# Second block's last linear layer by token halves: one in plain fp32 ahead of the row gathers, the other among the mixes

## The chip, the cores and the metric

The kernel runs on one core of one Trainium2 chip. The metric is the device time of one execution in microseconds (us), the median of several runs. Five engines work side by side, each on its own list of instructions and in order: TensorE (PE in the profile; PEld is its loading of weights), VectorE (DVE), ScalarE (ACT), GpSimd (POOL) and SyncE (SP). They wait for one another through semaphores only. Transfers are issued from SP (weights) and from POOL (gathered rows) into queues of their own, and the same 16 DMA engines serve both.

## The reference, cut to what matters

Two transformer blocks over 256 tokens of width 1024; the second block ends with a product-key expert layer (`peer`). What the change touches:

```python
# second_block, 256 tokens, D = 1024
merged = g_m * (y_m @ w_branch_mlstm) + g_l * (y_l @ w_branch_lru)
x = x + merged @ w_out                     # the last linear layer ahead of peer
h2 = rms_norm(x, norm2_g)
x = x + peer(h2, peer_w_q, sub_keys, expert_u, expert_v)

# peer, for 8 heads, 128 keys a half, 16384 experts
q = h2 @ w_q                               # 8 heads x 2 halves x 128
scores = q . sub_keys                      # 8 x 2 x 128 a token
idx, gate = the 16 best pairs of keys of each head, softmax
act = gelu(expert_u[idx] . h2)             # a row of 1024 for each index
out = sum over 8 x 16 of gate * act * expert_v[idx]
```

Each token needs 128 rows of `expert_u` and of `expert_v`, which lie side by side in DRAM as one row of 2048 floats (8 KB).

## The kernel before, in words

Activations lie with features on the 128 partitions: `hF` (the residual, named residual in the profile), `xF` (normed) and `merged` are 8 slices of 128 features by 256 tokens. Weights come in tiles of 1024 x 256 floats (1 MB), 2048 floats a partition, into a ring of seven slots (`raw_tiles`, weight_tiles in the profile). SP loads a tile (line 1475) when the tile seven places earlier has been freed by its last PE group. Products go through eight PSUM banks, four that DVE empties ("v") and four that ACT empties ("a"); `Groups.begin` makes PE wait until the bank's earlier content is taken.

*Split layers.* Linear layers whose rounding matters run in three passes of fp32r: ACT rounds a weight tile (`round_ahead`, line 1693, the activation at 1702), DVE makes the low part (`low_ahead`, lines 2290 to 2297), and `split_group` multiplies high x high, low x high and high x low over all 256 tokens (lines 734, 735, 738): 48 matmuls a tile. The activations are split likewise. Tiles are rounded up to two tiles ahead. *Plain layers* (queries, scores, keys) run in fp32 as they are; each such matmul leaves two records in the profile.

*Order around the change.* In `merge` PE computes branch_l in four groups; DVE multiplies each by a gate and adds it to merged (lines 3080, 3082); ACT rounds merged (line 2165) and DVE makes its low part (line 3086). PE then transposes the keys (keysT; DVE copies them, line 3092) and runs `w_out` as a split layer in four groups over all tokens. DVE adds each to the residual (line 2315), scales by the norm's gain into xF (`gained_rows`, line 2324), ACT squares (line 2171).

In `peer` (PE's from line 1329) the order is: head 0's query of token half 0 (line 1341), xF turned to token-major, scores of half 0 (line 1353), the same of half 1, sums of squares (`row_sums`, line 668), head 1's query (line 1364), the residual transposed into the output banks (line 1390). Then 257 batches of two row slots. For each: POOL gathers a row for each of 128 tokens (line 1678), DVE multiplies it with the tokens and sums (line 3198), ACT takes the gelu (line 2211), DVE makes a diagonal matrix (line 3208) and PE adds diagonal x row to the output banks (`mix`, line 1401). Eight batches make a unit (one head of one token half), 16 slots; eight units make a half. Written by hand between the mixes are: queries and scores of heads 2 to 7 on PE (`query`, two halves i of 16 matmuls over 256 tokens; `scores`, line 1378), their copies on ACT (lines 2175, 2179), the choice of keys and pairs for the unit two ahead on DVE. Head 0's first eight slots of half 0 get their index early (`early_rows`, line 3124); its last instruction, line 3154, releases POOL's first gather.

*Row buffers.* There are 16 buffers of 1 MB: four places outside the weight tiles, `squares`, three places of the rounded tiles, seven raw slots and `spare_row`. A raw slot can hold rows only after its last weight tile: buffer 8 + i is the slot of the query tile i + 1. `BUF_JOINS` says at which gather a buffer joins the rotation; until then it isn't used. Gather c waits for its index, and for the mix that used its buffer last (or for the tile's release).

Of the kernel before, what the change touches and what calls it, by code (L numbers as in the profile page):

```python
# [13 lines left out]
P = 128  # L14
# [29 lines left out]
BUF_JOINS = {9: 14, 10: 26, 11: 36, 12: 54, 13: 70, 14: 88}  # L44
# [187 lines left out]
def two_blocks(nc, t, out):  # L232
    with ExitStack() as ctx:
# [243 lines left out]
        g_m, merged = view(2048, KT, SEQ, extra=True), view(6272, KT, SEQ)  # L477
# [9 lines left out]
        merged_high, merged_low = x_high, by_k(work_parts[:, 6272:6272 + KT * SEQ])  # L487
# [104 lines left out]
        merged_rounded, merged_split = sem("merged_rounded"), sem("merged_split")  # L592
# [32 lines left out]
        def _(pe):  # L625
# [34 lines left out]
            def row_sums(key, parts=4):  # L660
# [655 lines left out]

            def merge():
# [9 lines left out]
                split_linear("w_out", "v", (arrived(merged_high, merged_rounded, 2), arrived(merged_low, merged_split, 2)))  # L1327

            def peer():
                x = normed()  # L1330
                query_slot = None

                def first_query(b):

                    nonlocal query_slot
                    if b == 0:
                        query_slot = G.plain_tile()
                    bank = G.begin("a", ("first_pq", b))
                    for k in range(KT):
                        for i in range(2):  # L1340
                            mm = pe.matmul(bank[:, i * P:(i + 1) * P], weight(query_slot)[:, k, i * P:(i + 1) * P],
                                           x(k)[:, b * P:(b + 1) * P], start=(k == 0 and i == 0), stop=(k == KT - 1 and i == 1))
                    G.end(mm)
                    if b == 1:
                        G.free()

                def first_scores(b):

                    pe.wait_ge(act_took, G.took["first_pq", b])
                    pe.wait_ge(dve_took, G.took["keysT", 0])  # L1350
                    bank = G.begin("a", ("first_scores", b))
                    for i in range(2):
                        mm = pe.matmul(bank[:, i * P:(i + 1) * P], qP[:, i, b * P:(b + 1) * P], keysT[:, i, :], start=True, stop=True)
                    G.end(mm)
# [1959 lines left out]
```

## Time and profile before

| | |
|---|---|
| median of 3 runs | 2529.25 us (2522.64 to 2538.05) |
| profiled execution | 2531.99 us, span of the profile 2530.2 us |
| busy in the span | PE 2362.8 us (93%), DVE 2022.8 (80%), ACT 1254.8 (50%), POOL 296.2 (12%) |
| DMA | 786.56 MB, mean 311 GB/s; SP's queue 504.46 MB, POOL's 276.58 MB |
| chain that ended last | PE 65%, DMA 17%, DVE 12%, ACT 3%, issue 3% |

The page cuts the span into 40 slices and gives the busy share of each engine in each; the windows give the same for any stretch, with the granted TensorE clock (1.00 is full speed), the share of the 16 DMA engines and GB/s. The chain that ended last goes from the last instruction back, at each step to what released it; "issue" is time in which nothing that the profile shows was waited for. Groups by form give count, total busy time and the mean of one instruction; matmuls overlap, so the pace of many is read from the total and not from the mean.

### The profile page before, as it was taken

How to read it: one execution, taken by the hardware profiler on the slowest of the kernel's cores; microseconds unless marked ns; L12 is line 12 of the kernel's file. 1: busy time of each engine (PE TensorE's matmuls, PEld its weight loads, DVE VectorE, ACT ScalarE, POOL GpSimd, SP SyncE). 2: the span in 40 equal slices, each digit the busy share in tenths (PEclk: the TensorE clock that was granted, in tenths of full speed). 3: DMA queues.
4: the chain of work that ended last, by engine and by line, in shares of the span. 5: the costliest groups of instructions: out<-in, count | busy, mean ns of one | idle time of the engine just before them, and what ended most of it. 6: DMA issues, size and time to landing. Idle time of an engine off the chain costs nothing.

```text
span 2530.2 us, 31600 instructions
## 1 busy us (share of the span) xinstructions
PE 2362.8 (93%) x12256; PEld 1864.8 (74%) x12256; DVE 2022.8 (80%) x3044; ACT 1254.8 (50%) x1303; POOL 296.2 (12%) x305
## 2 busy tenths in 40 slices
PE   9999999999899999999999999989999987878786
PEld 8899999899788788878878888988885543323332
DVE  5866764965899999999999998686768878787875
ACT  2564433264778888887888784438422111111111
POOL 0000000000000010000000000000023443333341
PEclk9999999999999999999999999999999999989899
DMA  8554555541999999999999996532679999999997
GB/s 245 163 190 131 190 195 150 159 151 35 403 363 394 421 408 406 421 414 414 408 417 412 407 414 202 149 101 90 223 275 416 421 421 421 422 422 421 421 421 299
DMA packets 238476, 786.56 MB, mean 311 GB/s; under 512 B 24368, under 2 KB 154544, under 8 KB 162288
## 3 DMA queue, kind: packets, MB, share of 16 engines
q1 hardware_dynamic: 198000, 504.46, 53.1%
q0 software_dynamic: 39184, 276.58, 26.7%
q10 hardware_dynamic: 1136, 3.43, 0.3%
q8 instruction: 99, 1.62, 0.3%
q14 instruction: 57, 0.47, 0.1%
HBM read 777.08 MB, written 7.34 MB: 310 GB/s over the span
## 4 chain that ended last, share of the span: by engine, by line
PE 65%; DMA 17%; DVE 12%; ACT 3%; issue 3%; POOL 0%; DVEq 0%; SPq 0%; ACTq 0%
DMA dense_weights<-in_peer_rows,work 13%; PE banks L914 7%; PE banks L915 7%; PE banks L916 7%; PE banks L734 6%; PE banks L735 5%; PE banks L738 5%; PE banks L1401 5%; PE banks L780 5%; PE banks L1026 3%; PE banks L1027 3%; DVE weight_tiles_low L2671 2%; DMA weight_tiles<-in_moe_tiles 2%; PE banks L644 1%; PE banks L1040 1%
## 5 line engine op out<-in xcount | busy, mean ns | idle before, releaser
L2671 DVE TENSOR_TENSOR weight_tiles_low<-weight_tiles,weight_tiles_high 128x2048 fp32r<-128x2048 f32 x212 | 481.3, 2286 | 32.8 <-ACT weight_tiles_high L1941 29.9
L1401 PE MATMUL banks<-dense_weights,work 128*128 128x512 f32 x888 | 412.8, 615 | 56.4 <-DVE work L3208 56.3
L1941 ACT ACTIVATE weight_tiles_high<-weight_tiles 128x2048 fp32r<-128x2048 f32 x207 | 396.2, 1918 | 81.7 <-PE banks L916 50.0
L1401 PEld LDWEIGHTS banks<-dense_weights,work 128*128 128x128 f32 x888 | 172.6, 198 | 286.8 <-issue 197.2
L2297 DVE TENSOR_TENSOR weight_tiles_low<-weight_tiles,weight_tiles_high 128x2048 fp32r<-128x2048 f32 x105 | 239.6, 2288 | 130.1 <-ACT weight_tiles_high L1702 129.8
L3198 DVE CUSTOM_DVE_ANT_0 dense_weights<-dense_weights,banks 128x1024 f32<-128x1024 f32 x222 | 266.5, 1218 | 67.1 <-DMA dense_weights<-in_peer_rows,work 66.1
L2211 ACT ACTIVATE work<-work,small 128x2 f32<-128x2 f32 x129 | 38.1, 295 | 538.5 <-DVE work L3198 538.1
L1678 POOL DMA_INDIRECT dense_weights<-in_peer_rows,work x222 | 208.9, 941 | 582.5 <-DVE work L3154 311.1
L734 PE MATMUL banks<-weight_tiles_high 128*128 128x256 f32 x992 | 235.8, 282 | 5.3 <-issue 4.4
L735 PE MATMUL banks<-weight_tiles_high,weight_tiles_low 128*128 128x256 f32 x992 | 233.1, 280 | 0.0
L1702 ACT ACTIVATE weight_tiles_high<-weight_tiles 128x2048 fp32r<-128x2048 f32 x105 | 200.2, 1909 | 58.0 <-PE banks L916 29.5
L734 PEld LDWEIGHTS banks<-weight_tiles_high 128*128 128x128 f32 x992 | 189.5, 191 | 8.7 <-issue 7.3
L735 PEld LDWEIGHTS banks<-weight_tiles_high,weight_tiles_low 128*128 128x128 f32 x992 | 189.4, 191 | 0.2
L914 PE MATMUL banks<-weight_tiles_high,gathered_parts 128*128 128x512 f32 x448 | 176.8, 395 | 1.7 <-DVE gathered_parts L2682 0.9
L1026 PE MATMUL banks<-weight_tiles_high,gathered_parts 128*128 128x512 f32 x448 | 176.5, 394 | 0.0
L916 PE MATMUL banks<-weight_tiles_high,gathered_parts 128*128 128x512 f32 x448 | 175.0, 391 | 0.0
L2671 DVE TENSOR_TENSOR work_parts<-work,weight_tiles_high 128x2048 fp32r<-128x2048 f32 x59 | 134.8, 2285 | 5.6 <-ACT weight_tiles_high L1941 5.3
L1941 ACT ACTIVATE weight_tiles_high<-work 128x2048 fp32r<-128x2048 f32 x59 | 113.6, 1925 | 30.7 <-PE banks L916 20.7
L3208 DVE TENSOR_SCALAR work<-ident,work 128x128 f32<-128x128 f32 x256 | 79.1, 356 | 47.8 <-ACT work L2211 46.8
L915 PE MATMUL banks<-weight_tiles_low,gathered_parts 128*128 128x512 f32 x296 | 115.5, 390 | 0.0
L780 PE MATMUL banks<-normed,weight_tiles 128*128 128x256 f32 (+1 forms) x512 | 111.7, 380 | 0.0
L1027 PE MATMUL banks<-weight_tiles_low,gathered_parts 128*128 128x512 f32 x280 | 109.2, 390 | 0.0
(543 smaller groups left out, 4855.1 us busy)
## 6 DMA issues: line engine op xcount, KB each, us to landing
weight_tiles<-in_moe_tiles SPq DMA_DIRECT2D x216, 1024.0 KB, 14.9
work<-in_moe_tiles SPq DMA_DIRECT2D x60, 1024.0 KB, 15.2
weight_tiles<-in_w_in SPq DMA_DIRECT2D x38, 1024.0 KB, 5.5
dense_weights<-in_moe_tiles SPq DMA_DIRECT2D x30, 1024.0 KB, 15.4
spare_row<-in_moe_tiles SPq DMA_DIRECT2D x30, 1024.0 KB, 15.3
weight_tiles<-in_w_xkv SPq DMA_DIRECT2D x16, 1024.0 KB, 5.4
weight_tiles<-in_ffn_w_gate SPq DMA_DIRECT2D x11, 1024.0 KB, 5.3
weight_tiles<-in_ffn_w_up SPq DMA_DIRECT2D x11, 1024.0 KB, 5.3
```

The source lines that it names most:

```text
L734: pe.matmul(o, high[:, k, n_], high_x(k), start=(k == 0 and i == 0), stop=False)
L735: pe.matmul(o, low[:, k, n_], high_x(k), start=False, stop=False)
L780: mm = pe.matmul(bank[0:m, i * SEQ:(i + 1) * SEQ], w[:, k, i * P:i * P + m], x(k), start=(k == 0), stop=(k == KT - 1))
L914: pe.matmul(o, a_high, b_high, start=start, stop=False)
L915: pe.matmul(o, a_high, b_low, start=False, stop=False)
L916: return pe.matmul(o, a_low, b_high, start=False, stop=stop)
L1026: pe.matmul(o, pairs, high, start=start, stop=False)
L1401: mm = pe.matmul(halves[half], diag[(first + j) % 8], pair_row(first + j)[:, 1, half * 512:(half + 1) * 512], start=False, stop=end and j ...
L1941: act.activation(high_tile(g, p, par, j), raw_tile(g, p, par, j), ACT.Copy).then_inc(g.high, 1)
L2297: dve.tensor_tensor(low_tiles[:, n % RING, 0:size], raw_tiles[:, n % RING, 0:size], high_tiles[:, j % HIGH_RING, 0:size].bitcast(F32), ALU ...
L2671: dve.tensor_tensor(low_tile(g, p, par, j), raw_tile(g, p, par, j), high_tile(g, p, par, j).bitcast(F32), ALU.subtract).then_inc(g.split, 1)
L3198: ins = dve.tensor_tensor_reduce(u_row, u_row, tokens(b), 1.0, 0.0, ALU.mult, ALU.add, dots[:, c:c + 1])
```

## The change

`w_out` no longer runs as a split layer. Its first half (tokens 0 to 127) runs in plain fp32 right after the keys, tile by tile; merged isn't rounded or split. Its second half (`out_rest`, tokens 128 to 255) follows among the mixes of unit 0, one tile ahead of the first mix and three behind mixes 3, 5 and 7; each group begins with identity x residual, so that ACT can copy the bank into the residual. The four tiles stay in their slots until then. Norm sums, roots and gains go by halves too (`row_sums`, `row_std_of`, `gained_rest`, `inverse_row_std`). Heads 0 to 3 (`HALVED`) get query and scores by halves: half 0 ahead of the mixes (heads 0 and 1) and in units 0 and 1 (heads 2 and 3), half 1 in units 2 to 5, their tiles held until then; heads 4 to 7 stay whole. merged moves to another place of the work area, and the joins of the row buffers change.

```diff
-BUF_JOINS = {9: 14, 10: 26, 11: 36, 12: 54, 13: 70, 14: 88}
+HALVED, SECOND_ORDER = 4, (1, 0, 2)
+BUF_JOINS = {11: 36, 12: 54, 8: 62, 13: 70, 14: 88, 9: 96, 10: 104}
...
-        g_m, merged = view(2048, KT, SEQ, extra=True), view(6272, KT, SEQ)
+        g_m, merged = view(2048, KT, SEQ, extra=True), view(8192, KT, SEQ)
...
 # PE, row_sums: one half at a time
-                    for b in range(TB):
-                        mm = pe.matmul(bank[:, b:b + 1], squares[:, k, b * P:(b + 1) * P], ones[:, 0:1],
-                                       start=(k == 0 and b == 0), stop=(k == KT - 1 and b == TB - 1))
+                    mm = pe.matmul(bank[:, 0:1], src[:, k, :], ones[:, 0:1], start=(k == 0), stop=(k == KT - 1))
...
 # PE, merge
-                split_linear("w_out", "v", (arrived(merged_high, merged_rounded, 2), arrived(merged_low, merged_split, 2)))
+                for g in range(4):
+                    out_tiles.append((G.plain_tile(), len(G.need) - 1))
+                    bank = G.begin("v", ("w_out", g))
+                    for i in range(2):
+                        for k in range(KT):
+                            pe.wait_ge(merged_ready, k // 2 + 1)
+                            mm = pe.matmul(bank[:, i * P:(i + 1) * P], weight(out_tiles[g][0])[:, k, i * P:(i + 1) * P], merged[:, k, 0:P],
+                                           start=(k == 0), stop=(k == KT - 1))
+                    G.end(mm, ("w_out", g))
...
 # PE, peer
+                def out_rest(g):
+                    slot, tile = out_tiles[g]
+                    bank = G.begin("a", ("w_out_rest", g))
+                    for i in range(2):
+                        o = bank[:, i * P:(i + 1) * P]
+                        pe.matmul(o, ident[:, :], hF[:, 2 * g + i, P:2 * P], start=True, stop=False)
+                        for k in range(KT):
+                            mm = pe.matmul(o, weight(slot)[:, k, i * P:(i + 1) * P], merged[:, k, P:2 * P], start=False, stop=(k == KT - 1))
+                    G.end(mm, ("w_out_rest", g))
+                    G.freed[tile] = (group_done, G.total)
...
-                first_query(0)
+                first_query(0, 0)
                 tokens("v", 0)
-                first_scores(0)
-                first_query(1)
-                first_scores(1)
-                row_sums("norm2_ms")
-                query(1, 0)
-                query(1, 1)
+                first_scores(0, 0)
+                first_query(1, 0)
+                row_sums(("norm2_ms", 0), squares[:, :, 0:P], 4)
+                first_scores(1, 0)
                 halves = [out_banks("v", 0)]
+                out_rest(0)
...
 # PE, behind the mixes (part is the batch within unit u)
                     if u == 0:
-                        if part == 0:
-                            scores(1)
-                        if part < 2:
-                            query(2, part)
+                        if part == 1:
+                            first_query(2, 0)
                         elif part == 2:
-                            scores(2)
-                        elif part in (4, 6):
-                            query(3, part // 2 - 2)
-                        elif part == 7:
-                            scores(3)
+                            first_scores(2, 0)
+                        elif part in (3, 5, 7):
+                            out_rest(part // 2)
+                    elif u == 1 and part == 0:
+                        first_query(3, 0)
                     elif h < PHEADS and part in (1, 3):
+                        if u == 1 and part == 1:
+                            first_scores(3, 0)
                         query(h, part // 2)
                     elif h < PHEADS and part == 5:
                         scores(h)
+                    elif u == 1 and part == 6:
+                        row_sums(("norm2_ms", 1), squares_rest, 1)
+                    elif 2 <= u < 2 + HALVED - 1 and part == 6:
+                        first_query(SECOND_ORDER[u - 2], 1)
+                    elif 3 <= u < 3 + HALVED - 1 and part == 0:
+                        first_scores(SECOND_ORDER[u - 3], 1)
+                    elif u == PHEADS - 3 and part == 1:
+                        first_query(HALVED - 1, 1)
+                    elif u == PHEADS - 3 and part == 3:
+                        first_scores(HALVED - 1, 1)
...
 # ACT, merge
-                for g in range(4):
-                    s = slice(2 * g, 2 * g + 2)
-                    round_ahead(("branch_l", g))
-                    act.wait_ge(merged_ready, g + 1)
-                    act.activation(merged_high[:, s, :], merged[:, s, :], ACT.Copy).then_inc(merged_rounded, 1)
+                round_ahead(("branch_l", 3))
...
 # ACT, behind gelu(n)
+                    elif u == 1 and part == 0:
+                        out_rest(3)
+                        act.wait_ge(act_took, G.took["w_out_rest", 3])
+                        act.activation(squares_rest, hF[:, :, P:2 * P], ACT.Square).then_inc(sq_ready, 1)
+                        first_query(3, 0)
...
 # DVE, merge
-                for g in range(4):
-                    s = slice(2 * g, 2 * g + 2)
-                    dve.wait_ge(merged_rounded, g + 1)
-                    dve.tensor_tensor(merged_low[:, s, :], merged[:, s, :], merged_high[:, s, :].bitcast(F32), ALU.subtract).then_inc(merged_split, 1)
...
-                add_to_residual("w_out", gained_rows)
+                for g in range(4):
+                    if g > 0:
+                        gained_rows(g - 1)
+                    ready(("w_out", g))
+                    s = hF[:, 2 * g:2 * g + 2, 0:P]
+                    take(dve.tensor_tensor(s, pair(bank_of(("w_out", g)), 2, P), s, ALU.add))
+                gained_rows(3)
...
 # DVE, behind weights(n)
-                    if u == 0 and part == 1:
+                    if u == 1 and part == 0:
+                        gained_rest()
+                    elif u == 2 and part == 1:
+                        inverse_row_std(1)
+                    elif u == 0 and part == 1:
                         choose_keys(1)
```

`first_query(h, b)` is the query of head h for token half b (16 matmuls of 128 columns), `first_scores(h, b)` its scores; a halved head's tile is freed by its second half. `gained_rest` waits for ACT's fourth copy of `out_rest` and scales the second half of the residual, eight instructions of 128 x 128.

## Rows read from the trace of the kernel before

**Rows 1.** The page, the span in 40 equal slices of 63.3 us: DMA share and GB/s.

```profile
DMA  8554555541999999999999996532679999999997
GB/s 245 163 190 131 190 195 150 159 151 35 403 363 394 421 408 406 421 414 414 408 417 412 407 414 202 149 101 90 223 275 416 421 421 421 422 422 421 421 421 299
```

**Rows 2.** Windows: stretch, length, busy time of each engine, clock, DMA share, GB/s.

```profile
1821.00:1839.00 18.00, 14.72 (x114) 14.27 (x114) 14.17 (x15) 6.68 (x5) 0.00 (x0) 0.91 0.54 176
1839.00:1865.00 26.00, 25.62 (x228) 25.42 (x226) 10.39 (x33) 5.47 (x8) 0.00 (x0) 1.00 0.52 162
1876.00:1926.00 50.00, 45.57 (x169) 29.21 (x167) 40.37 (x126) 8.85 (x18) 15.96 (x17) 1.00 1.01 422
1926.00:1936.00 10.00, 9.81 (x29) 4.99 (x30) 8.60 (x20) 4.45 (x8) 4.01 (x5) 1.00 0.98 385
2100.00:2500.00 400.00, 311.26 (x657) 129.49 (x656) 315.33 (x821) 54.46 (x123) 144.99 (x154) 0.92 1.01 421
```

**Rows 3.** Chain of waits, 1827 to 1881 us: start, us, what.

```profile
1828.70 0.66 PE banks L636 x4
1829.36 3.13 issue
...
1854.34 1.81 PE banks L738 x16
1856.15 3.57 PE banks L1341 x32
...
1881.40 3.44 PE banks L1401 x8
```

**Rows 4.** Timeline of DVE: start, us, engine, line, what, idle before and its releaser.

```profile
1825.76 2.29 DVE L2297 TENSOR_TENSOR weight_tiles_low<-weight_tiles,weight_tiles_high 128x2048 fp32r<-128x2048 f32 x1 [2.51 <-ACT weight_tiles_high L1702]
1829.29 2.49 DVE L3086 TENSOR_TENSOR work_parts<-work,weight_tiles_high 128x512 fp32r<-128x512 f32 x4
1831.70 2.47 DVE L3092 COPY work<-banks 128x512 f32<-128x512 f32 x4
...
1881.43 1.22 DVE L3198 CUSTOM_DVE_ANT_0 dense_weights<-dense_weights,banks 128x1024 f32<-128x1024 f32 x1 [1.25 <-DMA dense_weights<-in_peer_rows,work]
...
1886.58 0.76 DVE L3208 TENSOR_SCALAR work<-ident,work 128x128 f32<-128x128 f32 x2 [3.92 <-ACT work L2211]
```

**Rows 5.** Groups by form, 1827 to 1875 us: line, engine, what, count, busy, mean ns.

```profile
L1341 PE MATMUL banks<-normed,weight_tiles 128*128 128x128 f32 x64 | 7.5, 275 | 0.0
L1341 PEld LDWEIGHTS banks<-normed,weight_tiles 128*128 128x128 f32 x64 | 7.3, 192 | 0.0
...
L668 PE MATMUL banks<-ones,squares 128*128 128x1 f32 x32 | 4.7, 281 | 0.0
...
L2324 DVE TENSOR_SCALAR normed<-residual,cols 128x256 f32<-128x256 f32 x8 | 2.4, 349 | 0.0
```

**Rows 6.** Timeline of PE: half a head's query over 256 tokens.

```profile
1885.56 3.62 PE L1364 MATMUL banks<-normed,weight_tiles 128*128 128x256 f32 x16
```

**Rows 7.** Timeline of SP's queue: the second, fourth, seventh and eighth query tile.

```profile
1827.27 0.37 SPq L1475 DMA_DIRECT2D weight_tiles<-in_peer_w_q  x1
...
1839.86 0.37 SPq L1475 DMA_DIRECT2D weight_tiles<-in_peer_w_q  x1
...
1856.18 0.37 SPq L1475 DMA_DIRECT2D weight_tiles<-in_peer_w_q  x1
1864.65 0.37 SPq L1475 DMA_DIRECT2D weight_tiles<-in_peer_w_q  x1
```

**Rows 8.** Timeline of POOL: gathers 0, 25 and 255.

```profile
1865.81 1.00 POOL L1678 DMA_INDIRECT dense_weights<-in_peer_rows,work  x1 [311.11 <-DVE work L3154]
...
1930.16 0.94 POOL L1678 DMA_INDIRECT dense_weights<-in_peer_rows,work  x1 [6.79 <-PE banks L1401]
...
2488.13 0.94 POOL L1678 DMA_INDIRECT dense_weights<-in_peer_rows,work  x1 [0.30 <-issue]
```

**Rows 9.** Timeline of DVE: the product of the last row gathered.

```profile
2520.36 1.22 DVE L3198 CUSTOM_DVE_ANT_0 dense_weights<-dense_weights,banks 128x1024 f32<-128x1024 f32 x1 [0.53 <-DMA dense_weights<-in_peer_rows,work]
```

More of the change, by code:

```diff
@@ new lines, in peer, with x, first_query @@
+            def peer():
+                n_x = seen.next("x") - 1
+                query_slot, first_tiles = None, {}
+                def x(k, b=TB - 1):
+                    pe.wait_ge(x_ready, KT * (n_x + b) + k + 1)
+                    return xF[:, k, :]
+                def out_rest(g):
[8 more added lines that the diff above has]
+                    G.freed[tile] = (group_done, G.total)
+                def first_query(h, b):
@@ L1336, in first_query @@
                     if b == 0:
-                        query_slot = G.plain_tile()
-                    bank = G.begin("a", ("first_pq", b))
+                        first_tiles[h] = (G.plain_tile(), len(G.need) - 1)
+                    slot, tile = first_tiles[h]
+                    bank = G.begin("a", ("first_pq", h, b))
                     for k in range(KT):
                         for i in range(2):
-                            mm = pe.matmul(bank[:, i * P:(i + 1) * P], weight(query_slot)[:, k, i * P:(i + 1) * P],
-                                           x(k)[:, b * P:(b + 1) * P], start=(k == 0 and i == 0), stop=(k == KT - 1 and i == 1))
@@ L1343, in first_query @@
-                    G.end(mm)
+                            mm = pe.matmul(bank[:, i * P:(i + 1) * P], weight(slot)[:, k, i * P:(i + 1) * P],
+                                           x(k, b)[:, b * P:(b + 1) * P], start=(k == 0 and i == 0), stop=(k == KT - 1 and i == 1))
+                    G.end(mm, ("first_pq", h, b))
                     if b == 1:
[L1345 to L1351, printed above, removed]
+                        G.freed[tile] = (group_done, G.total)
@@ L1445, in peer @@
                         halves.append(out_banks("a", 1))
[L1446 removed]
+                G.row_freed = [None] * 4 + [(group_done, G.after["norm2_ms", 0])] + [None] * HIGH_RING + G.freed[keys_at + 2:] + [None]
             mlstm()
@@ L2211, in gelu @@
                     act.activation(acts[:, s], dots[:, s], ACT.Gelu, scale=row_rstd[:, b:b + 1]).then_inc(act_ready, 1)
-                for b in range(TB):
-                    ready(("first_pq", b))
-                    take(act.activation(qP[:, 0:2, b * P:(b + 1) * P], pair(banks_of(("first_pq", b)), 2, P), ACT.Copy))
-                    ready(("first_scores", b))
-                    take(act.activation(key_scores[:, b, 0:2, :], pair(banks_of(("first_scores", b)), 2, P), ACT.Copy))
-                ready("norm2_ms")
-                take(act.activation(row_std, banks_of("norm2_ms")[:, 0:TB], ACT.Sqrt, bias=EPS_AP, scale=1.0 / D))
+                first_query(0, 0)
+                first_scores(0, 0)
+                first_query(1, 0)
+                row_std_of(0)
+                first_scores(1, 0)
                 share(0)
+                out_rest(0)
                 for n in range(N_BATCHES):
@@ L2224, in peer @@
                     h = u + QUERY_AHEAD
-                    if n == HEAD_BATCHES:
-                        scores(3)
+                    if 3 <= u < 3 + HALVED - 1 and part == 1:
+                        first_scores(SECOND_ORDER[u - 3], 1)
                     if u == 0:
-                        if part == 0:
-                            query(1)
-                            scores(1)
-                        elif part == 2:
-                            query(2)
+                        if part == 2:
+                            first_query(2, 0)
                         elif part == 3:
-                            scores(2)
+                            first_scores(2, 0)
                             share(1)
+                        elif part in (4, 6):
+                            out_rest(part // 2 - 1)
                         elif part == 7:
-                            query(3)
                             share(AHEAD_UNITS)
+                    elif u == 1 and part == 0:
[3 more added lines that the diff above has]
+                        first_query(3, 0)
+                    elif u == 1 and part == 2:
+                        first_scores(3, 0)
                     elif part == 5 and h < PHEADS:
@@ L2242, in peer @@
                         scores(h)
+                        if u == 1:
+                            row_std_of(1)
+                        else:
+                            first_query(SECOND_ORDER[u - 2], 1)
                     elif part == 6 and u + AHEAD_UNITS < UNITS:
                         share(u + AHEAD_UNITS)
+                    elif u == PHEADS - 3 and part == 2:
+                        first_query(HALVED - 1, 1)
+                    elif u == PHEADS - 3 and part == 4:
+                        first_scores(HALVED - 1, 1)
                     elif part == 1 and u == PHEADS - 2 and G.pad_a:
```

52 lines of the change are left out of this document (34 added, 18 removed).

## The prediction

> **What bounds the kernel now.** The page's slices come first [rows 1]: the last ten of 40 slices, from about 1897 us, stand at a DMA share of 0.9 and 416 to 422 GB/s, and only the last falls off. In no view does an engine's busy share say as much: in the windows, PE is busy 78% and DVE 79% of 2100 to 2500 us, while DMA has a share of 1.01 at 421 GB/s [rows 2]. This is the stage of the row gathers: 256 indirect transfers of 128 rows of 8 KB, 1.049 MB each, which is 2.49 us at 421 GB/s. The first is issued at 1865.81 and waits for nothing but DVE's line 3154, the first index [rows 8]. The product of the last row starts when it lands, at 2520.36 [rows 9]; 9.8 us of tail follow. From first issue to last landing are 654.5 us, 2.5 us a gather with what little else is loaded. In the 26 us ahead, DMA has a share of only 0.52 [rows 2]. So two things set the end: when the first index is ready, and how many bytes still have to be moved after that. Time saved on PE, ACT or DVE behind 1866 us gives nothing while the queue holds gathers.
>
> **What leads up to the first index** is a chain on PE [rows 3]: keysT's last transposes at 1828.70, 3.13 us in which PE waits, then four groups of w_out up to 1856.15, then the first query (3.57 us). Keys, scores and indices behind it take 9.7 us more and are not changed by the edit.
>
> **The change, part by part.** (1) Start of w_out. Gone are four roundings of merged on ACT, its four low parts on DVE (2.49 us), and the splits of four w_out tiles; one of these (2.29 us at 1825.76) stands ahead of the last take of branch_l, and the 2.49 us stand ahead of the keysT copies, which free the banks [rows 4]. In their place w_out waits for the last sum of merged and for the first keysT copy. branch_l's last group ends at about 1827.1, just before SP's load that it frees, 1827.27 [rows 7]; take 0.69, sum 0.69, one copy 0.62 (a quarter of 2.47) make 1829.1, with hand-overs 1829.3 against 1832.49: **3.2 us** earlier.
>
> (2) w_out itself. Before: 1832.49 to 1856.15, 23.7 us. A split group lasts 5.44 us (three between the fourth and the seventh load, each freed by a group [rows 7]), four 21.8; the other 1.9 us are the clock: a mean of 0.91 over the 18 us to 1839 [rows 2] is some 3 us at 1.2 instead of 2.4 GHz, after PE's idle 3.13 us. The new pass has 16 plain fp32 multiplications of 128 columns a tile. Before has this very form in the first query: 32 records in 3.73 us (64 in 7.5) [rows 5]. Four tiles: 14.9 us, so **8.8 us** less. If the clock falls here too, up to 2.6 us come back; PE idles only some 0.7 us ahead, so I take full clock. Weight loads don't hold the plain pass up: 64 of them fill 7.3 us, 0.11 us each, beside matmuls at the same pace [rows 5].
>
> (3) The first query, tokens and scores of head 0 keep their order; the sum of the second two residual tiles and the gains (0.35 us each for 256 tokens [rows 5], now for 128) hide beside PE's 3.7 us. The first index comes **12.0 us** earlier, at 1853.8. Ends: 9.4 (half clock) to 12.6 (the gains shortened too).
>
> (4) Loads. Seven raw slots rotate. SP loads a query tile when the tile seven places before is free. Before, the fourth to seventh query tiles follow the four w_out groups: 1839.86 to 1856.18, all ahead of the gathers; only the eighth (1864.65) shares their time [rows 7]. Now w_out's tiles are held until their second half is done, so the fourth to seventh are issued at about 1862, 1894, 1905 and 1916, and the eighth at about unit 3, all among the gathers. **Four tiles move into the full stretch.** Price: 1839 to 1865 us has 4.2 MB, four tiles, at a share of 0.52 [rows 2], so 13.5 us of all 16 DMA engines, 3.4 us a tile. By bytes alone, at the gathers' 421 GB/s, it is 2.49. I take the row, 3.4, since it is this very transfer: **+13.5 us** (ends 10.0 and 13.8). The Trainium skill, *DMA: Bandwidth & Descriptors*, Specifications, puts line rate at pieces of 512 B and more, and these are of 1 KB; by that rule a tile would cost its bytes, 2.49 us, and the sum below would be -2.0 us. The row speaks against it.
>
> (5) Work moved among the mixes. PE gains 4 x 4.2 us (18 multiplications of 0.117 x 2), the queries of heads 1 to 3 in halves of 3.7 (same columns, smaller pieces), second norm sums (2.4, half of 4.7 [rows 5]); it loses head 1's whole query ahead of the mixes and a part of the norm sums. DVE gains 8 gains, between 1.4 and 2.8 us; ACT four copies (about 0.4 each), a square of 128 x 1024 and one root, 3 us. Cost **0**: DMA covers it, as long as POOL has gathers queued. ACT and DVE do wait in order: gained_rest waits for the fourth out_rest, behind it DVE's products; ACT's first_query(3,0) stands ahead of the next gelu. I count 8 us lost in unit 1 for both (4.5 until the out_rest is taken, then PE's mix and first query). In exchange the wait of 3.92 us for ACT at 1886.58 goes [rows 4].
>
> (6) Buffers. 9 instead of 10 to begin with, 9 against 12 just before gather 36, 11 against 14 just before gather 62, equal at 104. What counts is how many gathers are issued and not landed. Before, four have landed at 1881.4 [rows 4]; at 2.53 us each, 23.2 at 1930.16, when gather 25 is issued [rows 8]: under 2 queued, and the only dent of the stage is there, 0.98 and 385 GB/s over 10 us [rows 2], 0.9 us. After: first mix at 1866.5 (DVE's chain, not PE, releases it), unit 0 ends at about 1914, then 41.9 us of PE in unit 1 (eight mixes of 3.44 [rows 3], 3.7 + 0.5, two half queries of 3.45 [rows 6], 0.9, 2.4), with the waits 48. At 1948, 33 are issued; landed are 4 + (1948 - 1869.4 - 10.2)/2.53 = 31. Two are queued at the worst point, three or more elsewhere, since the moved loads slow the gathers down just there. Cost 0, with the dent of before as likely as not.
>
> **Sum**: -3.2 - 8.8 + 13.5 = **+1.5 us** on the profiled execution's 2531.99 (span 2530.2): 2533.5. That execution lies 2.7 above the median of the runs shown, 2529.25, so **2531**. The gain is real and is eaten by the loads. A measurement of this kernel tells about 0.5%, 12.6 us, from no change: I forecast no change.
>
> **Rivals.** *Starved queue, slower* (0.10): with 9 or 10 buffers mixes free them too late. Place: units 0 to 3. It decides when fewer than about 1.5 gathers are queued. For it: two is close; PE's work of units 0 to 4, some 205 us, is as much as the gathers' 80 x 2.53. If PE had the 0.92 clock of 2100 to 2500 us there, it would be 18 us late; less one gather of margin, +15: about 2546. Against it: in these units PE is near-always busy and granted 1.00 (1876 to 1926 [rows 2]).
>
> *Loads for free, faster* (0.06): if mixes rather than DMA pace the first units, SP's loads fill gaps. Then only the 12.0 to 12.6 and the dent of 0.9 count: 2516 to 2517. Against it: a share of 1.01 in 1876 to 1926.
>
> *The half pass isn't shorter* (0.04): weights of a plain pass load at half the speed in this order of operands, 0.22 us each in place of 0.11, so 29.8 us instead of 14.9 in line: -3.2 + 6.1 + 13.5, 2546. It decides once a group is over 5.9 us. Against it: the first query loads the same kind of tile at 0.11 [rows 5]. The Trainium skill has such a rule, *TensorE: Matmul & The Clock Gate*, section on weight-path perf modes: fast weight load, about a factor of 2 as measured, is on only where the input isn't FP32. The trace shows no such factor.
>
> *The tiles cost their bytes* (0.10): 4 x 2.49, the sum -2.0: 2527, still no change. The rule of the Trainium skill's DMA page above gives this.
>
> The forecast has the remaining 0.70. With the fourth, whose sign differs but not its verdict, it holds 0.80; their range, from -12.6 + 10.0 to -9.4 + 13.8 and 5 us of spread of the runs either way, is 2522 to 2539. With rivals to leave out no more than two in ten: 2520 to 2544. Faster by over 0.5%: 0.05, from the second rival and the spread; slower by over 0.5%: 0.11; same: 0.84.
>
> **What would show it.** Right: the first gather 12 us before its old time; w_out in four runs of 3.7 us at full clock; four more weight tiles landing behind the first gather; a share of 1.01 from there to the end; 668 us from first issue to last landing. Wrong: stretches under 1.0 between gathers 15 and 60 with POOL waiting for mixes (first rival); 654 us from first issue to last landing (second); w_out's groups more than 4 us apart (third); 664.5 us from first issue to last landing (fourth).

## The result and the profile after

The changed kernel takes 2536.61 us in the median (22 runs) against 2531.60 us before (22 runs beside them); the ratio is 1.0021 with a 95% interval of 1.0012 to 1.0029, so 5 us slower, between 3.0 and 7.3. That is within the 0.5% called no change, and within the range, though the interval leaves out 1: the kernel is slower by a little. Two executions far outside the rest, 13480.56 us of the kernel before here and 4124.97 us of e12 at a granted clock of 0.664, are left out of the ratios. The profiled execution has 2536.66 us and a span of 2534.9 us, 4.7 more than before.

The windows of the changed kernel (stretch, length, busy time of each engine, clock, DMA share, GB/s):

```profile
1840.00:1852.00 12.00, 12.00 (x110) 12.00 (x109) 2.88 (x13) 1.61 (x4) 0.00 (x0) 1.00 0.01 1
1852.00:1862.00 10.00, 10.00 (x91) 9.86 (x89) 9.27 (x48) 3.06 (x5) 5.26 (x6) 1.00 0.51 178
1876.00:1926.00 50.00, 45.98 (x234) 31.10 (x232) 38.24 (x114) 10.75 (x21) 15.08 (x16) 0.97 1.02 412
1926.00:1936.00 10.00, 8.71 (x34) 5.71 (x33) 7.19 (x27) 1.25 (x4) 1.87 (x2) 1.00 1.04 403
2040.00:2060.00 20.00, 11.04 (x31) 4.95 (x29) 13.89 (x40) 1.84 (x6) 5.61 (x6) 0.88 1.02 412
2060.00:2080.00 20.00, 13.91 (x42) 9.06 (x43) 12.50 (x34) 0.59 (x2) 3.21 (x4) 0.78 0.96 385
2080.00:2100.00 20.00, 20.00 (x81) 11.94 (x80) 8.96 (x20) 5.29 (x11) 7.11 (x8) 1.00 0.98 381
2100.00:2500.00 400.00, 318.93 (x719) 137.00 (x718) 321.66 (x849) 55.95 (x129) 154.05 (x164) 0.93 1.01 422
```

Beside [rows 2]: the stretch ahead of the gathers, which had a share of 0.52, now has 12 us with nothing to load at all, and there is a dent that before doesn't have, 0.96 and 0.98 at 2060 to 2100 us. The chain of waits from branch_l's end to the first gather:

```profile
1828.86 1.75 PE banks L636 x16
1830.61 0.41 issue
1831.02 14.53 PE banks L1333 x128
1845.55 3.57 PE banks L1365 x32
...
1855.21 0.99 POOL dense_weights L1711
```

PE waits 0.41 us ahead of w_out instead of 3.13, and the pass (line 1333, 128 records) is one unbroken piece of 14.53 us [rows 3]. The first gather is issued at 1855.21 instead of 1865.81, although this execution came to the end of branch_l 1.6 us later (1828.7 against 1827.1). Such an offset isn't the change's: in the profiles of this study whose code is that of before up to here, the first gather falls between 1862 and 1872 us. So I compare from branch_l's end on: 38.7 us to the first gather before, 26.5 after, **12.2 us** less. The product of the last row starts at 2525.03:

```profile
2525.03 1.22 DVE L3262 CUSTOM_DVE_ANT_0 spare_row<-spare_row,banks 128x1024 f32<-128x1024 f32 x1 [0.52 <-DMA spare_row<-in_peer_rows,work]
```

From first issue to last landing are 669.8 us against 654.5 [rows 8, 9], **15.3 us** more. -12.2 + 15.3 is +3.1 us for the change in this pair of traces (the spans differ by 4.7, of which 1.6 is the offset); the tail behind is the same to 0.1 us, 9.8 before and 9.9 after. The first 10 us behind the first issue differ too, before and after:

```profile
1865.81:1875.81 10.00, 10.00 (x47) 8.97 (x48) 9.40 (x39) 3.83 (x7) 7.58 (x8) 0.66 1.01 372
```

```profile
1855.21:1865.21 10.00, 6.85 (x61) 6.65 (x60) 9.40 (x39) 3.10 (x7) 7.56 (x9) 0.95 0.83 306
```

Before, the eighth tile, issued at 1864.65, is being loaded while the gathers start up; after, the next tile is issued only at 1862.09, and 0.18 of 10 us, 1.8 us of DMA, stay idle. The dent belongs to the eighth query tile; SP's issue, its landing in the DMA view (KB, us to landing), and PE's wait for it:

```profile
2040.32 0.37 SPq L1508 DMA_DIRECT2D weight_tiles<-in_peer_w_q  x1
```

```profile
weight_tiles<-in_peer_w_q SPq DMA_DIRECT2D x1, 1024.0 KB, 25.7
```

```profile
PE banks L1388 <- DMA weight_tiles<-in_peer_w_q: 15.0, 1, 15.0
```

### The profile page after: what moved, and what is told of

It is laid out like the page before. It is cut to its first block, busy times and chain, and to the rows that moved or that the text cites. A ratio compares the mean times of both kernels' runs of the same rounds, so it can differ in the third digit from the quotient of the medians.

```text
span 2534.9 us, 31965 instructions
## 1 busy us (share of the span) xinstructions
PE 2363.0 (93%) x12433; PEld 1875.9 (74%) x12433; DVE 2010.2 (79%) x3045; ACT 1249.5 (49%) x1310; POOL 296.1 (12%) x305
## 4 chain that ended last, share of the span: by engine, by line
PE 66%; DVE 14%; DMA 14%; ACT 3%; issue 2%; POOL 0%; ACTq 0%; DVEq 0%; SPq 0%
DMA dense_weights<-in_peer_rows,work 9%; PE banks L1425 7%; PE banks L912 7%; PE banks L914 7%; PE banks L913 7%; PE banks L778 5%; PE banks L732 5%; PE banks L736 5%; PE banks L733 5%; PE banks L1024 4%; PE banks L1025 4%; DMA weight_tiles<-in_moe_tiles 2%; DVE weight_tiles_low L2733 2%; DVE dense_weights L3262 2%; PE banks L1038 1%
## 5 line engine op out<-in xcount | busy, mean ns | idle before, releaser
L2733 DVE TENSOR_TENSOR weight_tiles_low<-weight_tiles,weight_tiles_high 128x2048 fp32r<-128x2048 f32 x212 | 481.6, 2289 | 33.4 <-ACT weight_tiles_high L1974 30.3
L1425 PE MATMUL banks<-dense_weights,work 128*128 128x512 f32 x872 | 401.4, 608 | 52.4 <-DVE work L3272 52.3
L1974 ACT ACTIVATE weight_tiles_high<-weight_tiles 128x2048 fp32r<-128x2048 f32 x207 | 396.3, 1919 | 82.3 <-PE banks L914 48.9
L1425 PEld LDWEIGHTS banks<-dense_weights,work 128*128 128x128 f32 x872 | 166.5, 195 | 270.0 <-issue 188.5
L2353 DVE TENSOR_TENSOR weight_tiles_low<-weight_tiles,weight_tiles_high 128x2048 fp32r<-128x2048 f32 x101 | 230.6, 2289 | 124.5 <-ACT weight_tiles_high L1735 124.2
L1735 ACT ACTIVATE weight_tiles_high<-weight_tiles 128x2048 fp32r<-128x2048 f32 x101 | 192.7, 1909 | 66.3 <-PE banks L736 33.5
L732 PE MATMUL banks<-weight_tiles_high 128*128 128x256 f32 x928 | 221.6, 283 | 2.4 <-issue 1.3
L733 PE MATMUL banks<-weight_tiles_high,weight_tiles_low 128*128 128x256 f32 x928 | 219.1, 280 | 0.0
L732 PEld LDWEIGHTS banks<-weight_tiles_high 128*128 128x128 f32 x928 | 176.0, 190 | 5.9 <-issue 4.0
L733 PEld LDWEIGHTS banks<-weight_tiles_high,weight_tiles_low 128*128 128x128 f32 x928 | 176.1, 190 | 0.2
```

Source lines behind the costliest of these rows:

```text
L732: pe.matmul(o, high[:, k, n_], high_x(k), start=(k == 0 and i == 0), stop=False)
L733: pe.matmul(o, low[:, k, n_], high_x(k), start=False, stop=False)
L1425: mm = pe.matmul(halves[half], diag[(first + j) % 8], pair_row(first + j)[:, 1, half * 512:(half + 1) * 512], start=False, stop=end and j ...
L1974: act.activation(high_tile(g, p, par, j), raw_tile(g, p, par, j), ACT.Copy).then_inc(g.high, 1)
L2353: dve.tensor_tensor(low_tiles[:, n % RING, 0:size], raw_tiles[:, n % RING, 0:size], high_tiles[:, j % HIGH_RING, 0:size].bitcast(F32), ALU ...
L2733: dve.tensor_tensor(low_tile(g, p, par, j), raw_tile(g, p, par, j), high_tile(g, p, par, j).bitcast(F32), ALU.subtract).then_inc(g.split, 1)
```

## The experiments

The theory at first: the 12 us are won and four loads of 3.4 us, moved into the full stretch, eat them. The rival: the loads cost little, and the mixes, with fewer row buffers, set the pace. Every ratio is to the kernel before on the same chip. Ratios are of many executions, gather times of one trace each. "Gather time" is from the first issue to the start of the last row's product, 654.5 us before and 669.8 after; it leaves out the spread of the 1850 us ahead.

**e1, small loads.** The changed kernel; of the fourth to seventh query tile only one eighth is loaded, so the queries of heads 3 to 6 aren't the reference's.

```diff
-            matrix(t["peer_w_q_2"][0])
+            w = t["peer_w_q_2"][0]
+            for h in range(PHEADS):
+                kts = 1 if 3 <= h <= 6 else KT
+                load((block_of(kts, 256), by_rows(w[0:kts * P, h * 256:(h + 1) * 256])))
```

> The changed kernel, but the fourth to seventh query tile (heads 3 to 6) are loaded by an eighth only; their queries work on what the slots held, so other rows are gathered, as many as ever. Theory 1 (the four tiles moved among the gathers cost 3.4 us of full DMA each): 4 x 3.4 x 7/8 = 11.9 us less than the changed kernel, so about 7 us faster than before, ratio 0.997. By bytes alone (2.49 us each) 8.7 us less, ratio 0.9985. Theory 2 (the loads are free; fewer row buffers starve the queue): no change against the changed kernel, ratio 1.002. A middle case: without the loads the mixes become the limit in units 0 and 1 and stretches of DMA share below 1.0 appear there, so that less than 8.7 us is won.

Measured: 1.0021 (1.0011 to 1.0031), the ratio of the changed kernel; gather time 675.1 us. The windows of e1 say why:

```profile
1890.00:1900.00 10.00, 10.00 (x50) 6.74 (x49) 7.67 (x24) 0.86 (x3) 2.15 (x3) 0.95 0.89 344
...
1930.00:1940.00 10.00, 9.63 (x33) 5.72 (x32) 8.49 (x28) 0.90 (x3) 3.75 (x4) 1.00 0.69 245
...
2070.00:2080.00 10.00, 10.00 (x28) 5.87 (x28) 3.14 (x8) 0.29 (x1) 1.88 (x2) 0.90 0.62 240
```

The bytes are gone, and DMA stands idle for at least as long. Where the changed kernel has 1.02 to 1.04, e1 has 0.69. (That the gather time of this trace is 5.3 us longer than the changed kernel's has no cause shown; the timed runs don't show it.) The theory, as I held it, falls: without the loads something else takes just as long. PE is near-always busy there and DVE waits, which points at the mixes.

**e2, the order of the second halves.** The slot of the eighth tile is free a unit earlier.

```diff
-HALVED, SECOND_ORDER = 4, (1, 0, 2)
-BUF_JOINS = {11: 36, 12: 54, 8: 62, 13: 70, 14: 88, 9: 96, 10: 104}
+HALVED, SECOND_ORDER = 4, (0, 1, 2)
+BUF_JOINS = {11: 36, 12: 54, 13: 70, 8: 78, 14: 88, 9: 96, 10: 104}
```

> The changed kernel with the second halves of heads 0 and 1 in the other order, so that the slot of head 0's tile is free a unit (40 us) earlier and the eighth query tile is loaded before PE wants it; buffer 8 joins at gather 78 instead of 62. Theory 1 with its late tile: PE's idle 15 us on the eighth tile and the dent of DMA at 2062 to 2102 go, 1.8 us less than the changed kernel, ratio 1.0014. Theory 2 (buffers): one buffer fewer for 16 gathers costs, or changes nothing: ratio 1.002 or more.

Measured: 1.0004 (0.9995 to 1.0012), 4 us less than the change by the ratios; gather time 668.4 us, 1.4 less. The eighth tile is issued at 2000.85, PE doesn't wait for it, and the dent is gone. The window of e2 where it was:

```profile
2060.00:2100.00 40.00, 39.78 (x158) 23.72 (x157) 31.73 (x86) 7.13 (x17) 17.00 (x18) 1.00 1.01 421
```

A buffer fewer for 16 gathers cost nothing that shows here. I had expected 1.8 us; the trace has 1.4 and the timed runs some 4, and as the two intervals just meet, the size is open.

**e3, the kernel before with the change's buffers.**

```diff
-BUF_JOINS = {9: 14, 10: 26, 11: 36, 12: 54, 13: 70, 14: 88}
+BUF_JOINS = {11: 36, 12: 54, 8: 62, 13: 70, 14: 88, 9: 96, 10: 104}
```

> The kernel before with the row buffers of the change (9 to begin with, joins at 36, 54, 62, 70, 88, 96, 104) and nothing else. Before had under 2 gathers queued at gather 25 by my reckoning, so one to three buffers fewer must starve it: theory 2 says that this alone makes the loss, 5 us or more, ratio 1.002 or more. Theory 1 says that the buffers cost here (dents of DMA share between 1900 and 1960, some 2 to 8 us, ratio 1.001 to 1.003), but not in the changed kernel, where the moved loads slow the gathers down; the trace of the changed kernel has its share at 1.01 to 1.04 there.

Measured: 1.0030 (1.0017 to 1.0042), 4 to 11 us slower by this line alone; gather time 658.7 us, 4.2 more, in an execution that lies 5.6 us below the median of e3. The windows of e3:

```profile
1890.00:1900.00 10.00, 7.34 (x23) 4.00 (x22) 9.19 (x25) 3.87 (x7) 1.87 (x2) 0.86 1.01 423
1900.00:1910.00 10.00, 10.00 (x32) 5.85 (x31) 8.64 (x29) 1.07 (x3) 3.76 (x4) 0.97 0.83 315
1910.00:1920.00 10.00, 10.00 (x32) 5.65 (x30) 8.85 (x29) 0.59 (x2) 3.79 (x4) 1.00 0.98 367
```

The queue does run short with 9 buffers. Both theories had given a number that the interval holds, so e3 doesn't choose between them. But the count of queued gathers was the right thing to look at, and the rival of a starved queue is a real mechanism of this kernel.

**e4, the second halves in line.** Each out_rest right behind its first half, ahead of the gathers; the slots are free and the fourth to seventh query tile load early again. The buffers stay as in the change.

```diff
 # PE, merge
                     G.end(mm, ("w_out", g))
+                    # the body of out_rest(g), written out here
...
 # PE, peer
-                out_rest(0)
...
-                        elif part in (3, 5, 7):
-                            out_rest(part // 2)
 # ACT, peer: each copy behind the square of the first half
```

> The changed kernel with the second half of each w_out tile right behind its first half, ahead of the gathers, so that the slots are free and the fourth to seventh query tile load ahead of the gathers again. Theory 1: first index 4 x 4.0 = 16 us later than in the changed kernel, loads of 13.5 us out of the full stretch, dent of 1.8 gone at best: between 0.5 and 2.5 us slower than the changed kernel, ratio 1.002 to 1.003. Theory 2: the first index 16 us later and nothing won: 16 us slower than the changed kernel, ratio 1.008.

Measured: 1.0068 (1.0051 to 1.0084), 17 us slower than before and 12 slower than the change. The first gather is issued at 1871.51, 16.3 us later than in the change; the gather time is 669.4 us, the same with four loads fewer. The windows of e4 have the idle DMA again:

```profile
1930.00:1940.00 10.00, 9.83 (x45) 6.21 (x43) 3.54 (x11) 0.13 (x1) 3.75 (x4) 0.90 0.69 251
1940.00:1950.00 10.00, 8.88 (x32) 5.83 (x33) 7.59 (x27) 1.11 (x4) 1.87 (x2) 1.00 0.93 361
1950.00:1960.00 10.00, 9.63 (x32) 5.52 (x31) 8.99 (x28) 0.59 (x2) 3.75 (x4) 1.00 0.81 290
```

My own theory's number, 1.002 to 1.003, missed; the rival's, 1.008, lies within the interval, and the trace is the rival's too: the first index 16 us later and nothing won. The mixes are slow here although no out_rest lies among them; the longest waits of e4 from 1880 to 1965 us are ACT's for head 3's first query and, behind it, PE's for DVE's diagonals, 9.9 and 9.8 us. With e1 this gave a third theory: in the changed kernel two limits of nearly the same length lie over each other in units 0 and 1, the bytes (gathers and loads) and the mixes with 9 buffers; taking one away gives nothing.

**e5 and e6: away with both.** e5 is e1 with the order of e2. e6 puts the work of units 0 and 1 where PE and DVE wait anyway:

```diff
 # PE; ACT's copies follow a batch behind
                 out_rest(0)
+                out_rest(1)
...
                         elif part == 2:
                             first_scores(2, 0)
-                        elif part in (3, 5, 7):
-                            out_rest(part // 2)
-                    elif u == 1 and part == 0:
-                        first_query(3, 0)
+                            out_rest(2)
+                        elif part == 4:
+                            out_rest(3)
+                        elif part == 6:
+                            first_query(3, 0)
+                    elif u == 1 and part == 0:
+                        first_scores(3, 0)
...
```

> The small loads of e1 together with the order of e2. In e1 the queue ran dry at 1890 to 1960 (shares of 0.69 to 0.99) and again behind the late eighth tile at 2070. With the order of e2 the second dent must go. If the mixes set the pace of units 0 and 1 whenever the loads don't (theory 3: two limits of nearly the same length), the first dent stays and the result is that of e2 at best: ratio 1.000, no gain from 3.67 MB fewer loads. Theory 1 pure: 11.9 us less than e2, ratio 0.9957.

> e5 with the work of units 0 and 1 put where PE and DVE wait: out_rest 1 ahead of the mixes, 2 behind mix 2, 3 behind mix 4, head 3's first query behind mix 6, its scores behind mix 8, and the copies of ACT a batch behind each. This takes the waits of DVE for out_rest 3 (5.2 us in e1's trace) and of ACT for head 3's query (5.5 us) out of unit 1; the buffers stay. Theory 3 with waits as the pace of the mixes: the first dent shrinks by 5 to 10 us against e5, ratio 0.996 to 0.998. If the 9 buffers are what limits, whatever the waits: less than 3 us.

Measured: e5 1.0008 (0.9999 to 1.0017), gather time 670.3 us; e6 0.9974 (0.9963 to 0.9985), gather time 660.4 us. The windows of e5:

```profile
1890.00:1930.00 40.00, 39.15 (x188) 25.90 (x188) 28.02 (x84) 9.94 (x19) 11.23 (x12) 0.92 0.93 362
1930.00:1960.00 30.00, 26.49 (x87) 15.17 (x87) 25.32 (x73) 4.97 (x13) 8.18 (x9) 1.00 0.87 322
```

and of e6:

```profile
1890.00:1930.00 40.00, 38.08 (x149) 22.47 (x148) 35.62 (x113) 9.19 (x20) 13.37 (x14) 1.00 1.00 411
1930.00:1960.00 30.00, 28.69 (x93) 15.51 (x93) 25.07 (x64) 8.53 (x15) 12.30 (x14) 1.00 0.98 389
```

Two waits of e5 in 1890 to 1960 us, of which e6 has only 1.8 us left:

```profile
ACT residual L2218 <- PE banks L1353: 20.3, 3, 7.7
...
ACT work L2206 <- PE banks L1365: 5.5, 1, 5.5
```

ACT stood before PE's out_rest and head 3's query with the gelus queued behind it, hence DVE's diagonals, hence the mixes, hence the buffers. e6 has 9.9 us less gather time than e5, and 8.0 less than e2, which has both the waits and the loads; the buffers are the same. By the ratios it is 8.6 and 7.6 us. e6 is faster than the kernel before, but three and a half tiles of its queries are never loaded. The third theory holds. Few buffers and waits are one limit, not two: fewer buffers leave less room for a wait.

**e7 and e8: tiles in 8 KB pieces.** The host lays the query weights out tile by tile, as it does the experts' weights; e7 is e2 with this, e8 the kernel before.

```diff
-            matrix(t["peer_w_q_2"][0])
+            for h in range(PHEADS):
+                load((lambda s: s, t["peer_w_q_2"][h]))
```

> The kernel of e2 with the query weights laid out on the host tile by tile, so that a load's pieces are 8 KB in place of 1 KB; same bytes. Five loads lie in the full stretch. If a tile costs 3.4 us for its pieces and 2.5 us for its bytes, 4.5 us less than e2 as long as DMA is the limit, ratio 0.9985. If the mixes are as long (theory 3), the time won turns into dents of DMA share around 1930 and less than 2 us are won.

> The kernel before with the same layout of the query weights. Only the eighth tile shares the time of the gathers, so 0.9 us at most: ratio 1.000. In the windows ahead of the gathers four tiles then need a smaller DMA share than 0.52 over 26 us: 0.39 if a tile costs its bytes.

Measured: e7 1.0008 (0.9998 to 1.0018), gather time 669.8 us, no gain over e2: time won on loads is lost to the mixes, as its window has it:

```profile
1935.47:1945.47 10.00, 9.62 (x29) 5.16 (x28) 9.06 (x26) 0.59 (x2) 3.43 (x4) 1.00 0.87 334
```

e8 1.0011 (1.0002 to 1.0020), gather time 654.4 us. So the layout by itself took 0.5 to 5 us more in the timed runs, where I had expected at most 0.9 less; the gather time is the same, and what it costs elsewhere stays open. The share of e8 ahead of the gathers was 0.47 over 26 us for the same bytes, not 0.39. That would be 3.1 us a tile, where e12 below shows 2.4; so a share read where one tile loads alone isn't the price in a full stretch, and in both layouts it is too high.

**e9 and e10: the best version.** e9 is e2 with the placing of e6; e10 has the 8 KB pieces too.

> The changed kernel with the order of e2 and the placing of e6, full loads. DMA is full in e2, so fewer waits alone should give nothing unless e2's queue was short somewhere: 0 to 2 us less than e2, ratio 0.9995 to 1.0005; the time from first issue to last landing stays at 666 to 668 us.

> e9 with the query weights in 8 KB pieces. With the waits out of the mixes and the cheaper loads both limits move: 3 to 5 us less than e9, ratio 0.998 to 0.999, faster than both kernels. If the 9 buffers hold the mixes' pace, no more than 1 us less than e7.

Measured: e9 1.0005 (0.9992 to 1.0017), gather time 669.5 us; e10 1.0000 (0.9989 to 1.0012), gather time 665.7 us. DMA is full throughout in e10 (1.01 and 421 GB/s at 1890 to 1960 us). The 3.8 us that I expected between e9 and e10 are in the traces, but the intervals overlap; "faster than both kernels" missed. e10 has the lowest ratio of the kernels that compute the whole, with intervals that don't tell it from e2 or e9, and it equals the kernel before.

*What sets the pace of the mixes.* The gathers are issued as the mixes free buffers, so the issue of gather 33, near the end of the worst stretch, tells how fast the mixes were. Three of these rows, of the changed kernel, e1 and e6:

```profile
1949.79 0.94 POOL L1711 DMA_INDIRECT dense_weights<-in_peer_rows,work  x1 [4.71 <-PE banks L1425]
1948.38 0.94 POOL L1714 DMA_INDIRECT dense_weights<-in_peer_rows,work  x1 [4.71 <-PE banks L1425]
1941.87 0.94 POOL L1716 DMA_INDIRECT dense_weights<-in_peer_rows,work  x1 [4.71 <-PE banks L1425]
```

Counted from gather 0 of each trace:

| | all loads | small loads |
|---|---|---|
| before; e3 (its buffers only) | 80.7; 87.5 us | |
| work placed as in the change | 94.6 (change), 94.7 (e2), 97.0 (e7) | 96.5 (e1), 96.5 (e5) |
| work placed as in e6 | 87.7 (e9), 89.0 (e10) | 86.4 (e6) |

The buffers alone make gather 33 some 7 us later. The placing of the work adds another 7 to 10. The four loads add nothing. That is what two limits over each other look like: in the changed kernel the mixes hold the gathers back, and the four tiles fill the gaps that this leaves. With the waits gone the loads do have their price: from e9 to e6, 669.5 to 660.4, it is 9.1 us for three and a half tiles, 2.6 us each.

**e11 and e12: the price of a load by itself.** The kernel before with four more tiles, one after the other, into a place that is free then, far behind units 0 and 1; nothing reads them. e12 has the 8 KB pieces.

```diff
             sp.wait_ge(act_took, G.took["key_scores", PHEADS - 1])
+            for h in range(4):
+                sp.dma_start(work[:, 0:TILE_F].rearrange("p (k n) -> p k n", k=KT),
+                             by_rows(t["peer_w_q_2"][0][:, h * 256:(h + 1) * 256])).then_inc(gain_loaded, 16)
+                sp.wait_ge(gain_loaded, 16 * (h + 1))
```

> The disputed price by itself: the kernel before, with four more loads of 1 MB tiles of the query weights (pieces of 1 KB) one after the other behind head 7's scores, at about 2075 us, where ten and more gathers are queued; nothing reads them. Kernel before has 654.5 us from first issue to last landing. 3.4 us a tile (the share of before): 668.1, ratio 1.0054. By bytes, 2.5 us: 664.5, ratio 1.004. Less, if pieces of the loads fill gaps of the gathers: 658, ratio 1.0015. The landing of one takes 13 to 26 us.

> The same four extra loads with the query weights laid out in 8 KB pieces. By bytes 664.5 us from first issue to last landing, ratio 1.004; the difference to e11 is the price of the pieces, 3.6 us if e11 shows 668.1, none if e11 shows 664.5.

Measured: e11 1.0047 (1.0032 to 1.0062), gather time 666.2 us: 11.7 more, **2.9 us a tile**. e12 1.0036 (1.0023 to 1.0049), gather time 664.0: 9.6 more than e8, **2.4 us a tile**, its bytes. The ratios of both agree (12 and 9 us more than before) but overlap, so the difference of 0.5 us rests on a trace each; the mean of 414 GB/s in e11's view against 421 in e12's, at full engines in both, points the same way. The DMA view of e11, 2070 to 2190 us (packets, MB, share; then the landing):

```profile
q0 software_dynamic: 6180, 45.02, 90.7%
q1 hardware_dynamic: 4253, 4.58, 11.1%
...
work<-in_peer_w_q SPq DMA_DIRECT2D x4, 1024.0 KB, 25.7
```

and of e12:

```profile
q0 software_dynamic: 6287, 45.77, 91.7%
q1 hardware_dynamic: 720, 4.72, 9.5%
...
work<-in_peer_w_q SPq DMA_DIRECT2D x4, 1024.0 KB, 9.0
```

A tile in 1 KB pieces takes 25.7 us to land, one in 8 KB pieces 9.0. Packets of SP's queue are 1.1 KB in e11 and 6.6 KB in e12, POOL's 7.3 KB in both. If the two queues take turns packet by packet, a tile of 1024 pieces waits for 1024 gather packets, (1 + 8) KB each turn, 22 us at 421 GB/s; one of 128 pieces for 128, 5 us; both are some 3 to 4 us short of the measured landings. This reckoning fits roughly, and was only argued. The Trainium skill, *DMA: Bandwidth & Descriptors*, Queues, rings and completion order, has each engine go round-robin between queues at packet granularity. The landings agree with turns that go by pieces and not by bytes; how many pieces make a turn no row here shows.

## Why the prediction was right or wrong

*What bounds the kernel.* Right: two things set the end, the first index and the bytes behind it. Incomplete: in units 0 and 1 of the changed kernel the mixes are a third, as long as the bytes; e1, e5, e6 and the issue of gather 33 show it.

*(1) Start of w_out, 3.2 us.* Branch_l's end to w_out's start: 5.4 us before, 2.3 after, 3.1 less. Right.

*(2) The pass, 14.9 in place of 23.7.* 14.5, at full granted clock. Right; the row of the first query carried over to 128 records. The rival of slow fp32 weight loads, for which I named the Trainium skill, *TensorE: Matmul & The Clock Gate*, section on weight-path perf modes, didn't come: 128 loads in 14.4 us, 0.11 us each, here too.

*(3) The first index, 12.0 us.* 12.2. Right.

*(4) The loads, +13.5 us.* That four tiles move was right (SP issued them at 1862, 1897, 1908 and 1919 us against my 1862, 1894, 1905, 1916). The price was too high: 2.9 us a tile by e11, so 11.7. I had taken the share of a stretch where tiles load one at a time. e11 and e12 lie 0.5 us apart, so pieces of 1 KB do seem to cost something, half of what I gave them. By the rule of the Trainium skill, *DMA: Bandwidth & Descriptors*, Specifications, line rate from 512 B on, the estimate was 2.5 us: the rule is off by about as much as my row, the other way.

*(5) Work among the mixes, cost 0; (6) buffers, cost 0.* Half right. DMA stayed at 1.02 to 1.04 there, and gather 33 was issued at 1949.8 against my 1948. But I had counted two queued there and three or more elsewhere. POOL's queue had moved 33.59 MB by then, 32.0 of the 33 gathers issued, and 16.98 MB, 16.2 of 17, when gather 17 was issued at 1901.16. So 1.0 and 0.8 were queued or under way, below the 1.5 that I had named as the mark of a starved queue. The "0" held only because the tiles' bytes kept DMA busy meanwhile; it isn't a property of the work or the buffers (e3: 4.2 us of gather time in the kernel before). The 8 us of waits that I had counted in unit 1 are in that 1948; what I missed altogether lies in unit 0.

*What the sum left out.* First the eighth tile. I wrote that it is loaded at about unit 3 and never asked how long a tile takes to land among gathers: 25.7 us, where it is wanted some 10 us later. PE waited 15 us, POOL 21 for PE, and the dent followed. e2 takes it away: 1.4 us by the trace, some 4 by the runs. Then the start: before, the eighth tile fills 1.8 us of DMA that stand idle behind the first issue in the changed kernel. Of the 15.3 us more gather time 11.7 are the four tiles by e11's price, 1.8 the start and 1.4 the late tile; 0.4 is left, less than one trace can tell. e10 fits: it has no late tile and no dent, but the same share of 0.83 in its first 10 us, and keeps 1.6 us over four tiles at 2.4. In units 0 and 1 the changed kernel has no dent.

*The sum.* +1.5 predicted, +3.1 in this pair of traces, +5.0 timed. No change was right; the sign too. That 669.8 us came so near my 668 is in part luck: the price of the loads was 1.8 us too high, and 3.6 us were left out. The reason given ("the gain is eaten by the loads") is right for the ledger and wrong as a cause by itself: taking the loads out gives nothing while the waits stay.

*The rivals.* Starved queue: its condition was met, its price wasn't; it is what bounds the kernel once the loads are gone. Loads for free: half its mechanism is there, the tiles do fill gaps of the gathers, but the mixes that leave these gaps take as long, so nothing is won; and each tile costs 2.9 us where DMA alone is the limit. Tiles at the price of their bytes: the sum would be -2.0; measured are 669.8 us and not 664.5, and 2.9 a tile.

## What to carry to other kernels

Where a transfer queue is the limit, read a change as two numbers, when the queue starts and what it has to move from then on; a tile that no longer loads in idle time is paid in full wherever that queue alone is the limit. Before naming one cause of a loss, take it out and look whether another of the same length lies below: here neither the loads nor the waits alone gave anything, both together 8 us. And give a load that shares its engines with a deep queue of large pieces its landing time from a row of that situation, not from an idle one.

## What the runs showed of the hardware that was not expected

A 1 MB tile in 1 KB pieces landed 25.7 us after its issue beside full-rate gathers of 8 KB rows, one in 8 KB pieces after 9.0, and 5.5 (median) with DMA partly idle. The time that they added to the gathers differed by far less, 2.9 against 2.4 us a tile, from one trace each. Also the share of the DMA engines in a partly idle stretch, 0.52 for 162 GB/s in 1 KB pieces and 0.47 in 8 KB pieces, which is 3.4 and 3.1 us a tile, overstates what the same loads took from a full one.
